# Attention with the probabilities turned three items and multiplied four items behind the scores, instead of two and three

## The reference, cut to what matters

```
o = g[..., 0:1] * o_cmp + g[..., 1:2] * o_slc + g[..., 2:3] * o_win
```

## Time and profile before

| | |
|---|---|
| median of 3 runs | 2728.56 us (2726.22 to 2728.69) |
| the profiled execution | 2727.86 us |
| its span, first to last instruction | 2726.1 us |
| PE busy, share of the span | 97% |
| DVE, ACT busy | 68%, 51% |
| the attention stage, first S to the first product of `out1` | 1724.0 to 1833.7 us |
| PE, DVE, ACT busy in 1763 to 1824 us (61 us) | 52.72, 52.17, 41.19 us |

### The profile page before, as it was taken

The page is one execution under the profiler, slowest core; times in us unless marked ns, Lnnn a source line. Parts: engine busy times, 40 slices in busy tenths (PEclk is TensorE's granted clock), DMA queues, the critical chain, the costliest instruction groups (busy, mean ns, idle before and its releaser), DMA issues.

```text
span 2726.1 us, 42735 instructions
## 1 busy us (share of the span) xinstructions
PE 2641.1 (97%) x16064; PEld 2328.7 (85%) x16064; DVE 1857.0 (68%) x2686; ACT 1394.7 (51%) x1866; POOL 145.6 (5%) x149
## 2 busy tenths in 40 slices
PE   7999999999999999999989999889999999999999
PEld 7999888888888888888778888668888888888887
DVE  4699856667765775677755666775677757775775
ACT  5588655346634553454433444553456535543553
POOL 0001100210000000002100000001100000000003
PEclk9999999999999999999988999999999999999999
DMA  6454334555555555554745566105555555555554
GB/s 215 155 186 140 119 110 152 185 193 185 186 191 193 185 185 190 193 183 166 216 137 159 173 190 192 48 3 186 198 183 187 185 185 191 192 188 185 189 174 147
DMA packets 238536, 464.50 MB, mean 170 GB/s; under 512 B 12506, under 2 KB 14170, under 8 KB 238426
## 3 DMA queue, kind: packets, MB, share of 16 engines
q1 hardware_dynamic: 236922, 460.73, 50.8%
q10 hardware_dynamic: 1504, 2.29, 0.3%
HBM read 460.90 MB, written 2.10 MB: 170 GB/s over the span
## 4 chain that ended last, share of the span: by engine, by line
PE 86%; DVE 5%; DMA 4%; ACT 3%; issue 1%; SPq 0%; DVEq 0%; ACTq 0%
PE bank L1706 47%; PE bank L1709 23%; PE bank L1952 4%; PE bank L1953 4%; PE bank L1954 4%; DVE weight_tail L1069 2%; ACT weight_head L603 2%; DMA weight_raw<-in_cd_w_in 1%; PE bank L1988 1%; DMA weight_raw<-in_ffn_w_up 1%; DMA w<-in_nsa_cmp_w 1%; PE bank L1892 1%; PE bank L2031 1%; DMA weight_raw<-in_ab_w_out 0%; DMA weight_raw<-in_cd_w_out 0%
## 5 line engine op out<-in xcount | busy, mean ns | idle before, releaser
L1069 DVE TENSOR_TENSOR weight_tail<-weight_raw,weight_head 128x2048 fp32r<-128x2048 f32 (+1 forms) x456 | 1000.1, 2193 | 772.9 <-ACT weight_head L603 771.2
L603 ACT ACTIVATE weight_head<-weight_raw 128x2048 fp32r<-128x2048 f32 (+1 forms) x456 | 832.1, 1825 | 982.3 <-DMA weight_raw<-in_ffn_w_up 313.2
L1706 PE MATMUL bank<-norm_in,weight_head 128*128 128x512 f32 x3840 | 1211.8, 397 | 11.1 <-DVE residual L1422 6.5
L1709 PEld LDWEIGHTS bank<-norm_in,weight_tail 128*128 128x128 f32 x3840 | 723.8, 188 | 171.4
L1709 PE MATMUL bank<-norm_in,weight_tail 128*128 128x256 f32 x3840 | 756.7, 278 | 0.0
L1706 PE MATMUL bank<-mixed,weight_head 128*128 128x512 f32 x2176 | 700.9, 396 | 6.5 <-DVE mixed L1483 3.7
L1706 PEld LDWEIGHTS bank<-norm_in,weight_head 128*128 128x128 f32 x3840 | 587.3, 189 | 13.2 <-DVE weight_tail L1069 7.4
L1709 PEld LDWEIGHTS bank<-mixed,weight_tail 128*128 128x128 f32 x2176 | 410.1, 188 | 80.4
L1709 PE MATMUL bank<-mixed,weight_tail 128*128 128x256 f32 x2176 | 462.4, 280 | 0.0
L1706 PEld LDWEIGHTS bank<-mixed,weight_head 128*128 128x128 f32 x2176 | 347.0, 189 | 26.4 <-DVE residual L1422 5.1
L1952 PE MATMUL bank<-norm_in,weight_head 128*128 128x256 f32 x896 | 261.0, 291 | 5.3 <-ACT zx L842 5.3
(11 more groups left out here) (287 smaller groups left out, 1546.8 us busy)
## 6 DMA issues: line engine op xcount, KB each, us to landing
weight_raw<-in_ffn_w_up SPq DMA_DIRECT2D x176, 1024.0 KB, 4.9
weight_raw<-in_ffn_w_down SPq DMA_DIRECT2D x64, 1024.0 KB, 5.0
weight_raw<-in_cd_w_in SPq DMA_DIRECT2D x64, 1024.0 KB, 5.7
weight_raw<-in_ab_w_in SPq DMA_DIRECT2D x56, 1024.0 KB, 4.9
weight_raw<-in_ab_w_out SPq DMA_DIRECT2D x32, 768.0 KB, 4.4
weight_raw<-in_ffn_w_down SPq DMA_DIRECT2D x32, 768.0 KB, 4.2
weight_raw<-in_cd_w_out SPq DMA_DIRECT2D x32, 768.0 KB, 4.1
x_stage<-in_x SPq DMA_DIRECT2D x4, 512.0 KB, 5.8
```

Source lines behind the costliest of these rows:

```text
L603: act.activation(WHEAD[:, off % RING, 0:kt * CW], WRAW[:, off % RING, 0:kt * CW], ACT.Copy)\
L1069: dve.tensor_tensor(WTAIL[:, off % RING, 0:kt * CW], WRAW[:, off % RING, 0:kt * CW], WHEAD[:, off % RING, 0:kt * CW].bitcast(F32), ALU.sub ...
L1706: pe.matmul(bank[c][:, :], head, rhs[:, u * s.kt + k, :], start=u == 0 and k == 0, stop=False)
L1709: mm = pe.matmul(bank[c][:, 0:SEQ], tail, rhs[:, u * s.kt + k, 0:SEQ], start=False, stop=u == s.units - 1 and k == s.kt - 1)
```

## The change

T moves one loop back on PE, from T(n-2) to T(n-3), and O from O(n-3) to O(n-4). ACT's K moves with T. S(n) now waits for K(n-4). There are four `prob` buffers, so A(n) waits for T(n-4); the buffers move to a free part of the same arena. H and C move from even loops (n = 2h + 6) to odd ones (n = 2h + 7), and the loops run one turn longer. The turned compressed branch of item m goes to bank 2 + m % 2 instead of 3 - m % 2. Even items' scores of both long branches are one matmul of 2 x 128 columns where there were two of 128. The wait of O for C(h-2) is unchanged.

```diff
+PROBS = 4
...
-        PROB = at("prob", places["norm_in"] + 8192, [P, 3, 528], F32)
+        PROB = at("prob", places["norm_in"] + 22528, [P, PROBS, 528], F32)
...
# ACT
-            for n in range(last + 5):
+            for n in range(last + 6):
...
-                if 2 <= n < last + 2:
-                    m = n - 2
+                if 3 <= n < last + 3:
+                    m = n - 3
...
-                if n >= 6 and n % NT == 0:
+                if n >= 7 and n % NT == 1:
                     h = n // NT - 3
                     act.wait_ge(o_done, NT * (h + 1))
...
# DVE
-                    if n >= 3:
-                        dve.wait_ge(pt_done, n - 2)
+                    if n >= PROBS:
+                        dve.wait_ge(pt_done, n - PROBS + 1)
...
-                if n >= 6 and n % NT == 0:
+                if n >= 7 and n % NT == 1:
                     h = n // NT - 3
                     dve.wait_ge(o_head, h + 1)
...
# PE
-                    if n >= 3:
-                        pe.wait_ge(pt_read, 2 * (n - 2))
+                    if n >= 4:
+                        pe.wait_ge(pt_read, 2 * (n - 3))
...
-                        for r in range(2):
-                            pe.matmul(bank[b][:, r * SEQ:r * SEQ + P], qh, BC[:, 2 * g + r, 0:P], start=True, stop=True)
+                        pe.matmul(bank[b][:, :].rearrange("p (r k) -> p r k", r=2)[:, :, 0:P], qh, BC[:, 2 * g:2 * g + 2, 0:P],
+                                  start=True, stop=True)
...
-                if 2 <= n < items + 2:
-                    m = n - 2
+                if 3 <= n < items + 3:
+                    m = n - 3
...
                     pe.wait_ge(pn_ready, 3 * (m + 1))
-                    pe.wait_ge(s_read, min(m + 2, items))
+                    pe.wait_ge(s_read, min(m + 3, items))
...
-                if n >= 3:
-                    m = n - 3
+                if n >= 4:
+                    m = n - 4
```

More of the change, by code:

```diff
@@ L1027, in _ @@
                     act.activation(PT[:, m % 2, 0:blocks * P], bank[4 + m % 2][:, 0:blocks * P], ACT.Copy).then_inc(pt_read, 1)
-                    act.activation(PTC[0:NCMP, m % 2, :], bank[3 - m % 2][0:NCMP, P:2 * P], ACT.Copy).then_inc(pt_read, 1)
+                    act.activation(PTC[0:NCMP, m % 2, :], bank[2 + m % 2][0:NCMP, P:2 * P], ACT.Copy).then_inc(pt_read, 1)
                 if n < last:
-                    b, p3, nk = n % 2, n % 3, P * (n % NT + 1)
+                    b, p3, nk = n % 2, n % PROBS, P * (n % NT + 1)
                     act.wait_ge(mx_ready, n + 1)
@@ L1622, in branches @@
                 return a.rearrange("p (r k) -> p r k", r=2)[:, :, 0:nk]
-            for n in range(items + 5):
+            for n in range(items + 6):
                 if n in (6, 10):
@@ L1630, in _ @@
                     nk = P * (t + 1)
-                    p3 = PROB[:, n % 3, :]
-                    if n >= 3:
-                        dve.wait_ge(pt_done, n - 2)
+                    p3 = PROB[:, n % PROBS, :]
+                    if n >= PROBS:
+                        dve.wait_ge(pt_done, n - PROBS + 1)
                     dve.wait_ge(s_done, n + 1)
@@ L1656, in _ @@
                     for r in range(2):
-                        pr = PROB[:, m % 3, r * SEQ:r * SEQ + nk]
+                        pr = PROB[:, m % PROBS, r * SEQ:r * SEQ + nk]
                         dve.tensor_scalar(pr, pr, FAC[:, 4 * b + 1 + r:4 * b + 2 + r], None, ALU.mult).then_inc(pn_ready, 1)
-                    pr = PROB[:, m % 3, 512:512 + NCMP]
+                    pr = PROB[:, m % PROBS, 512:512 + NCMP]
                     dve.scalar_tensor_tensor(out=pr, in0=pr, scalar=FAC[:, 4 * b:4 * b + 1], in1=CMP1[:, t, :],
@@ L2019, in _ @@
             items = NSA_HEADS * NT
-            for n in range(items + 3):
+            for n in range(items + 4):
                 if n < items:
@@ L2051, in _ @@
                             pe.transpose(bank[4 + b][:, i * P:(i + 1) * P],
-                                         PROB[:, m % 3, r * SEQ + kb * P:r * SEQ + (kb + 1) * P], IDENT[:, :])
+                                         PROB[:, m % PROBS, r * SEQ + kb * P:r * SEQ + (kb + 1) * P], IDENT[:, :])
                             i += 1
-                    pe.transpose(bank[3 - b][0:NCMP, P:2 * P], PROB[:, m % 3, 512:512 + NCMP], IDENT[:, :]).then_inc(pt_done, 1)
-                if n >= 3:
-                    m = n - 3
+                    pe.transpose(bank[2 + b][0:NCMP, P:2 * P], PROB[:, m % PROBS, 512:512 + NCMP], IDENT[:, :])\
+                      .then_inc(pt_done, 1)
+                if n >= 4:
+                    m = n - 4
                     b, (h, t) = m % 2, divmod(m, NT)
```

## The result

The changed kernel takes 2740.15 us (median of 9 runs, 2736.73 to 2746.02) and the kernel before 2728.98 us (median of 9, 2725.12 to 2734.15): a ratio of 1.0038, 95% interval 1.0026 to 1.005. Two more comparisons on other chips gave 1.0042 (1.0028 to 1.0055) and 1.0032 (1.0017 to 1.0047). It is some 10 us slower, outside the forecast range. The profiled execution took 2741.34 us, its span 2739.6 us against 2726.1.

What follows compares the result with a forecast made beforehand. A cycle through PE and DVE, B(even), T(even), O(odd), S(odd), A(odd), was taken to set the 6.09 us turn. Terms of -2.75, +0.36, +0.14, +3.5 and +2.13 gave +3.4 us, hence 2731.5 us, range 2726 to 2735.5.

Steps and rivals of the forecast that it cites:

- What bounds the kernel now: Steady part: the cycle B(even), T(even), O(odd), S(odd), A(odd) sets the 6.09 us turn, DVE's own cycle close behind at about 6.0.
- H and C in odd loops, and what is late next: Steady turn: C ends 3.91 us in, O(even) waits for it, A(odd) follows 2.53 later; 6.44 us against 6.09.
- a covered product: Rival, 18%: the wait of O(even) for C is covered, a turn is DVE's 6.04 us; -1.2 us, 2727.
- a DVE that no longer waits for H: Rival, 9%: H runs before E(odd) ends, a turn is 5.36 us, 12 turns save 8.8 us; about 2717.
- One matmul of 2 x 128 columns: Even items' scores on PE: the merged matmul lies in PE's slack or under a wait; zero.
- The end: From A(31) to the first product of `out1`: 11.01 us against 8.88, +2.13 us.
- The start: Stage start: A(3) follows B(1) directly and C(0) is no longer ahead of A(7), which comes 2.75 us earlier.
- the rival that the start gives nothing back: Rival, 12%: S(4), T(1), S(5) at half clock delay A(4) or A(5); only 0.86 us gained, +5.3 us, 2733.3.
- The clock: Rival, 7%: PE's pause of over 1 us a turn lowers its steady-part clock; 12 to 24 us, 2743 to 2755.
- The sum: Whole stage: -2.75, +0.36, +0.14, +3.5 and +2.13 make +3.4 us, giving 2731.5 us.
- a sign of being wrong: Profile after: turns of 6.1 us or less, a clock below 1.00 after 1743, or a product never waiting for C.

Runs made afterwards that it cites:

- the run with the split in even loops: The changed kernel with H and C put back into even loops (n = 2h + 6), all else as changed: ratio 0.9987, median 2732.44 us.
- the faster kernel: The changed kernel with H and C back in even loops and H ahead of E there: ratio 0.9945, median 2720.79 us.

## Why the prediction was wrong

*What bounds the kernel now*: right. The run with H first in the kernel before kept 6.09 us, with PE's chain in front. One reading was off: DVE's own cycle is 2.81 + 0.52 + 0.34 + 2.21 = 5.88 us by the prediction's own rows (5.87 in the run with the split in even loops), not about 6.0, so 0.2 us a turn was to be won, not 0.05 to 0.1. The forecast doesn't use it.

*H and C in odd loops, and what is late next*: right. C was forecast to end 3.91 us into a turn and ended at 3.90; from there to A(odd) 2.53 was forecast and 2.54 came; the turn is 6.44 as worked out. The rivals with a covered product or a DVE that no longer waits for H did not occur.

*One matmul of 2 x 128 columns*: right, nothing.

*The end*: 11.01 us forecast. In the trace T(30) starts 5.09 us after A(31), as forecast (5.08); what follows took 7.48 us instead of 5.93. The excess lies around the window with the clock at 0.56: the products of an odd item, for one, took 1.78 us from 1838.12 on, for 1.06 at the full clock.

*The start*: half right. A(3) came without its wait for the scores, but A(7) came 1.64 us earlier (22.96 us after A(0) for 24.60), not 2.75: S(5) took 2.08 us at the slow clock, and A(5) waited 1.05 us for it. This is part of the rival that the start gives nothing back.

```profile
1741.09 2.08 PE L2032 MATMUL bank<-bc,zx 128*128 128x512 f32 x2
...
1743.51 0.17 DVE L1636 TENSOR_TENSOR prob<-bank,cmp_mask 128x15 f32<-128x15 f32 x1 [1.05 <-PE bank L2036]
```

*The clock*: this is the step that failed. The sum has the slow clock of the steady part and of the end at nothing. It was a rival with a chance of 7%, dismissed because 1.00 was granted throughout the steady part with PE idle 8 of 61 us, and a clock below 1.00 after 1743 was named as a sign of being wrong; it came at 1770. The change moved PE's idle time into one pause of 1.1 us a turn and made it larger, and the clock fell for one to three turns at a time and at the end. The rival's price was wrong too: all twelve turns slow, 12 to 24 us, where in truth a few are.

The sum closes. Forecast for the stage +3.4 us; the slow clock added 1.11 at the start, 0.52, 1.56 and 1.82 in three turns (6.96, 8.00 and 8.26 less 6.44), and 1.56 at the end, together 6.57. 3.4 + 6.57 = 9.97, and 117.98 - 108.02 = 9.96 us was measured. The remaining 3.5 us between the two spans lie outside the stage (A(0) 1.6 us later, the rest 1.9 us longer). In seventeen traces A(0) lies anywhere from 1723.0 to 1728.5 us though the steps ahead of it are the same, so these 3.5 us can't be put down to the change.

The same sum fits the changed kernel with idle matmuls, where the clock is at 1.00 behind the start: 108.02 + 3.4 + 1.11 at the start, less 0.7 for turns of 6.38 us, plus 0.76 for an end of 11.77 us (one idle matmul stands in its path), is 112.6 us, and 112.60 and 112.62 were measured.

In time, the idle matmuls gave back 8.9 us on one chip. The stages say the same: 117.98, 119.69 and 122.99 us in the three traces of the changed kernel, 112.60 and 112.62 in the two with the idle matmuls, so 5.4 to 10.4 us by the execution. What the idle matmuls themselves add (0.76 us) and take (0.7 us) about cancels. The clock is thus the larger part of what the change costs: its ratio to the kernel before falls from 1.0032 to 1.0008. The kernel before varies as well: its stage took 108.02 us in the trace that the prediction read and 111.26 in the other. Why the clock falls in one turn and not in the next like it is open.

The Trainium skill (TensorE: Matmul & The Clock Gate, "A second HAM failure mode: psum-queue depth-cycling") tells that short pauses between groups of matmuls can make the clock swing; the prediction set this aside since the trace of before disagreed. The traces after agree with it: pauses of 1.1 us a turn, and the clock between 0.50 and 1.00.

## What to carry to other kernels

When a step is moved by one turn of a loop that treats even and odd items differently, see what it now stands in front of: the wait for C kept its distance, but it came to block the long scores with the short half of DVE's work as cover, and was moved back at no cost. Put the small operation that others wait for (H, 0.36 us) ahead of the long one it doesn't depend on, but only once the chain that really bounds the turn is out of the way: alone it gave nothing, with the later turning it gave half a per cent. And when a change leaves PE idle longer at one place, a clock of 1.00 in one trace of before is no proof: look at several traces, and at PE's thinnest stretch.

## What the runs showed of the hardware

- Work added to PE made the kernel faster: fourteen idle matmuls of 1.02 us each took 8.9 us off the changed kernel (2742.16 to 2733.26 us).
- A fall came behind PE's thinnest stretch in all three traces of the changed kernel (turn from A(11); PE busy 3.66 of 6 us ahead of it in the first) and in the one with the split in even loops (turn from A(13)); the steady part of the faster kernel, where the turns leave PE hardly a pause, had none. The kernel before had none from A(11) to A(31) in either of its traces, but one between A(7) and A(11) in the second. Thin stretches are not all of it: the fall behind A(25) in the first trace came in a stretch of 6 us (1809 to 1815) with PE busy 4.87, and the stretches 1785 to 1791 and 1791 to 1797, also at 4.87 of 6, had none.
- A matmul that waited for C started 0.15 us after C's end in the kernel before and in the changed one, and 0.06 us after it where an idle matmul stood right in front of its wait. PE's idle time did not decide it: 0.18 us of it went with 0.15 in one kernel and with 0.06 in the other.
- The profile named as the releaser of a product a copy that the product doesn't ask for; it had ended within 0.03 us of the real releaser. Where two come so close, hold the name against the counts in the code.
